# A two-block layer kernel: five changed waits in the first block, three weight low halves by an adding DMA, six selection rounds inside the sparse attention

## What is computed

```python
proj = h @ w_in                                   # h: normed, modulated x, [512, 1024]
ssm_u, ssm_z, q, k, v, attn_z, q_idx, k_idx, w_idx = jnp.split(proj, split_points, axis=-1)
y_ssm = s5_mixer(ssm_u, ...) * jax.nn.silu(ssm_z)     # a state space scan, then a gated linear unit
# dsa_mixer: score = sum over 8 index heads of w_idx * relu(q_idx . k_idx), causal;
#            the 128 best keys of each query; softmax(q . k / 8 + bias) over those keys; times v
y_attn = dsa_mixer(q, k, v, q_idx, k_idx, w_idx, ...) * jax.nn.silu(attn_z)
x = x + gate * (jnp.concatenate([y_ssm, y_attn], -1) @ w_out)
```

## Time and profile before

| | |
|---|---|
| median of 3 runs | 1530.57 us (1530.06 to 1534.65) |
| span of the profiled execution | 1522.9 us |
| TensorE busy | 1484.2 us (97%) |
| VectorE busy | 828.6 us (54%) |
| ScalarE busy | 604.1 us (40%) |
| GpSimd busy | 20.7 us (1%) |
| mean granted TensorE clock | 0.996 of full speed |

### The profile page before, as it was taken

The page is one execution under the profiler, slowest core; times in us unless marked ns, Lnnn a source line. Parts: engine busy times, 40 slices in busy tenths (PEclk is TensorE's granted clock), DMA queues, the critical chain, the costliest instruction groups (busy, mean ns, idle before and its releaser), DMA issues.

```text
span 1522.9 us, 19833 instructions
## 1 busy us (share of the span) xinstructions
PE 1484.2 (97%) x8104; PEld 1203.6 (79%) x8104; DVE 828.6 (54%) x1359; ACT 604.1 (40%) x918; POOL 20.7 (1%) x36
## 2 busy tenths in 40 slices
PE   8999999999999999999999999999999999999997
PEld 6766957668887887888889777888887888888887
DVE  7978987775646663334346343433448544443234
ACT  4355335663336553334336333432334323232220
POOL 0020100000000000000000000000000000000000
PEclk9999999999999999999999999999999999999998
DMA  9531533043221112122222212223331323232221
GB/s 351 174 112 57 115 130 121 28 166 139 99 79 72 56 56 68 71 83 84 100 102 84 84 56 83 83 83 111 138 111 56 111 83 111 83 111 77 104 97 56
DMA packets 24905, 151.69 MB, mean 100 GB/s; under 512 B 3520, under 2 KB 6128, under 8 KB 8800
## 3 DMA queue, kind: packets, MB, share of 16 engines
q1 hardware_dynamic: 22304, 136.71, 24.9%
q0 software_dynamic: 2512, 13.72, 3.3%
HBM read 143.83 MB, written 7.88 MB: 100 GB/s over the span
## 4 chain that ended last, share of the span: by engine, by line
PE 86%; DVE 10%; ACT 2%; issue 1%; DMA 1%; SPq 0%; DVEq 0%; ACTq 0%
PE bank L574 84%; DVE score L2206 1%; DVE small L2205 1%; DMA w_raw<-wstream 1%; PE bank L1021 1%; DVE w_lo L1958 1%; DVE score L2221 1%; DVE tval L1911 1%; PE bank L953 0%; DVE sgb L1918 0%; DVE y_lo L1984 0%; DVE h_lo L1984 0%; DVE tval L2455 0%; ACT w_hi L1288 0%; DVE sgb L2322 0%
## 5 line engine op out<-in xcount | busy, mean ns | idle before, releaser
L574 PE MATMUL bank<-h_hi,w_hi 128*128 128x512 f32 (+1 forms) x1104 | 438.4, 397 | 6.6 <-DVE w_lo L1958 3.1
L574 PE MATMUL bank<-h_hi,w_lo 128*128 128x512 f32 (+1 forms) x1120 | 437.0, 390 | 0.0
L574 PE MATMUL bank<-h_lo,w_hi 128*128 128x512 f32 (+1 forms) x1104 | 430.6, 390 | 0.0
L1958 DVE TENSOR_TENSOR w_lo<-w_raw,w_hi 128x2048 fp32r<-128x2048 f32 (+2 forms) x104 | 234.6, 2256 | 248.9 <-ACT w_hi L1288 247.2
L1288 ACT CAST w_hi<-w_raw 128x2048 fp32r<-128x2048 f32 (+2 forms) x108 | 202.6, 1876 | 139.0 <-PE bank L574 134.8
L574 PEld LDWEIGHTS bank<-h_hi,w_hi 128*128 128x128 f32 (+1 forms) x1104 | 207.1, 188 | 62.3 <-issue 17.9
L574 PEld LDWEIGHTS bank<-h_hi,w_lo 128*128 128x128 f32 (+1 forms) x1120 | 210.3, 188 | 45.3
L574 PEld LDWEIGHTS bank<-h_lo,w_hi 128*128 128x128 f32 (+1 forms) x1104 | 207.3, 188 | 41.6 <-issue 0.2
L574 PE MATMUL bank<-y_hi,w_hi 128*128 128x512 f32 x272 | 108.9, 400 | 1.9 <-DVE y_lo L1984 1.9
L574 PE MATMUL bank<-y_hi,w_lo 128*128 128x512 f32 x272 | 106.1, 390 | 0.0
L574 PE MATMUL bank<-y_lo,w_hi 128*128 128x512 f32 x272 | 105.9, 389 | 0.0
(11 more groups left out here) (401 smaller groups left out, 1821.0 us busy)
## 6 DMA issues: line engine op xcount, KB each, us to landing
w_raw<-wstream SPq DMA_DIRECT2D x119, 1024.0 KB, 4.8
w_raw<-wstream SPq DMA_DIRECT2D x4, 768.0 KB, 4.2
bias_rows<-bias_table POOLq DMA_DIRECT2D x1, 2560.0 KB, 11.2
xr<-xT SPq DMA_DIRECT2D x4, 512.0 KB, 5.2
bias<-bias_rows POOLq DMA_DIRECT2D x1, 2048.0 KB, 12.8
xr<-xT SPq DMA_DIRECT2D x1, 2048.0 KB, 8.4
x_saved<-xr POOLq DMA_DIRECT2D x1, 2048.0 KB, 10.8
xr<-x_saved POOLq DMA_DIRECT2D x1, 2048.0 KB, 8.0
```

Source lines behind the costliest of these rows:

```text
L574: return pe.matmul(out, lhsT, rhs, start=start, stop=stop)
L1958: dve.tensor_tensor(w_low_of(s)[:, 0:kt, :], w_raw[:, i % RAW_SLOTS, 0:kt, :], hi_of(s)[:, 0:kt, :].bitcast(f32), ALU.subtract).then_inc(w ...
```

## The change

1. VectorE: `split_low(2)` stands ahead of `state_inputs`, `split_low(3)` ahead of `input_rows(1)`, `split_low(4)` right behind `chunk_turns`; `output_rows` in two parts around `split_low(5)`.
2. The transposes of `win_re` follow the first tile of `ssm_u`, those of `win_im` stand between the halves of the second, through four banks; ScalarE's copies are moved accordingly.
3. Each quarter of the scan's outputs waits for its own `k_ready` instead of for the fourth.
4. Gate tiles 2, 3 and 4: VectorE's `gate_low` is gone. ScalarE writes the negated high half (as it is rounded on the way out) over the raw half, and GpSimd issues a DMA, two for each tile, that adds the weights from HBM to it. TensorE waits for both DMAs of a tile before it uses it.
5. `silu(az)` becomes x/2 * (1 + tanh(x/2)): ScalarE computes tanh per part (j = 0, 2, 4, 6), VectorE `(tanh + 1) * x` (j = 2, 3, 6, 7), and `attn_gated` multiplies by 0.5 as well; it moves from j = 9 to 10, its low half from 10 to 11.
6. Six of the eleven rounds behind `k_ready` move into the attention, at j = 2, 4, 5, 6, 8 and 9.

```diff
@@ GpSimd, behind the load of the bias
+            for j, n in enumerate(NEGATED):          # NEGATED = (2, 3, 4)
+                i = SPLIT_AT[GATE_TILES[n].s]
+                for part in range(2):
+                    ks = slice(4 * part, 4 * part + 4)
+                    pool.wait_ge(gate_negated, 2 * j + part + 1)
+                    pool.dma_start(w_lo[:, i % RAW_SLOTS, ks, :],
+                                   wstream[i].rearrange("p (t c) -> p t c", c=WC)[:, ks, :],
+                                   accum_op=ALU.add).then_inc(gate_summed[j], 16)
@@ TensorE, gemm_unit, k == 0
+                    if gr in GATE_TILES and GATE_TILES.index(gr) in NEGATED:
+                        pe.wait_ge(gate_summed[NEGATED.index(GATE_TILES.index(gr))], 32)
@@ TensorE, ssm_u
-            for gr in G["ssm_u"]:
-                gemm(gr, "fm", h_hi, h_lo)
-            pe.wait_ge(win_ready, 1)
-            for b in range(8):
-                src = (win_re, win_im)[b // 4]
-                if b >= 2:
-                    pe.wait_ge(wint_act, b - 1)
+            def input_turns(part):
+                if part == 0:
+                    pe.wait_ge(win_ready, 1)
+                src = (win_re, win_im)[part]
+                for b in range(4):
+                    if part:
+                        pe.wait_ge(wint_act, b + 1)
...
+            gemm(G["ssm_u"][0], "fm", h_hi, h_lo)
+            input_turns(0)
+            gemm(G["ssm_u"][1], "fm", h_hi, h_lo, between=lambda: input_turns(1))
@@ TensorE, the scan's outputs
-            pe.wait_ge(k_ready, 4)
...
             for q in range(4):
+                pe.wait_ge(k_ready, q + 1)
@@ TensorE, ahead of out1
+            pe.wait_ge(gate_summed[-1], 32)
@@ ScalarE, ssm_u
             for w, gr in enumerate(G["ssm_u"]):
                 ahead(gr)
+                if w:
+                    input_turned(0)
...
                     elif half == 0:
                         cosine(cos_t[:, :, :]).then_inc(rotation_ready, 1)
+                        input_turned(1)
@@ ScalarE, gate_high
+                act.activation(w_low_of(s)[:, ks, :], w_raw[:, i % RAW_SLOTS, ks, :], ACT.Copy, scale=-1.0)\
+                   .then_inc(gate_negated, 1)
@@ ScalarE, attention
+            def gate_tanh(m):
+                if m >= 2:
+                    act.wait_ge(tanh_used, m - 1)
+                act.activation((root, rstd)[m % 2][:, :], az[:, m, :], ACT.Tanh, scale=0.5).then_inc(tanh_ready, 1)
...
-                if j == 7:
-                    gate_silu(az, range(4))
-                if j == 9:
+                if j == 10:
                     attn_high(0)
                     attn_high(1)
@@ VectorE, the start
+            split_low(2)
             state_inputs()
             input_rows(0)
-            split_low(2)
+            split_low(3)
             input_rows(1)
             dve.nop().then_inc(win_ready, 1)
-            split_low(3)
             chunk_turns()
+            split_low(4)
...
-            output_rows(0, 1)
-            split_low(4)
-            output_rows(1, 3)
+            output_rows(0, 2)
             split_low(5)
-            output_rows(3, 4)
+            output_rows(2, 4)
@@ VectorE, behind k_ready
-            select_keys(11)
+            select_keys(11 - len(SELECTED))          # SELECTED = (2, 4, 5, 6, 8, 9)
@@ VectorE, attention
+            def gate_finished(m):
+                dve.wait_ge(tanh_ready, m + 1)
+                dve.scalar_tensor_tensor(out=az[:, m, :], in0=(root, rstd)[m % 2][:, :], scalar=1.0, in1=az[:, m, :],
+                                         op0=ALU.add, op1=ALU.mult).then_inc(tanh_used, 1)
...
+                if j == 2:
+                    dve.nop().then_inc(w_low, len(NEGATED))
+                if j in SELECTED:
+                    select_keys(1)
+                if j in GATE_FINISHED:               # {2: 0, 3: 1, 6: 2, 7: 3}
+                    gate_finished(GATE_FINISHED[j])
```

More of the change, by code:

```diff
@@ L36 @@
 BIAS_LEN = 640
+NEGATED = (2, 3, 4)
 D_FF = 2816
@@ L309, in hybrid_blocks @@
         ki_copied, ki_doubled, wi_ready, wi_row, wi_psum, mod_row, gate_row = sem("ki_copied"), sem("ki_doubled"), sem("wi_ready"), sem("wi_row"), sem("wi_psum"), sem("mod_row"), sem("gate_row")
-        az_ready = sem("az_ready")
+        az_ready, tanh_ready, tanh_used = sem("az_ready"), sem("tanh_ready"), sem("tanh_used")
         x_act, kr_psum, k_ready, heads_loaded = sem("x_act"), sem("kr_psum"), sem("k_ready"), sem("heads_loaded")
@@ L328, in hybrid_blocks @@
         sc_psum, a_ready, o_psum, o_copied = sem("sc_psum"), sem("a_ready"), sem("o_psum"), sem("o_copied")
-        gate_ready = sem("gate_ready")
+        gate_ready, gate_negated = sem("gate_ready"), sem("gate_negated")
+        gate_summed = [sem(f"gate_summed{j}") for j in range(len(NEGATED))]
         on_ready, dec_loaded = sem("on_ready"), sem("dec_loaded")
@@ L467, in hybrid_blocks @@
         GATE_HIGH = {2: (2, 0), 3: (2, 1), 6: (3, 0), 7: (3, 1), 11: (4, 0), 12: (4, 1)}
-        GATE_LOW = {0: ((1, 0), (1, 1)), 1: ((1, 2), (1, 3)), 4: ((2, 0), (2, 1)), 5: ((2, 2), (2, 3)),
-                    8: ((3, 0), (3, 1)), 9: ((3, 2), (3, 3)), 13: ((4, 0), (4, 1)), 14: ((4, 2), (4, 3))}
+        GATE_LOW = {0: ((1, 0), (1, 1)), 1: ((1, 2), (1, 3))}
+        SELECTED = (2, 4, 5, 6, 8, 9)
         GATE_UNITS = [4] * 8 + [3] * 8
         GATE_DONE = {0: 0, 2: 1, 4: 2, 6: 3, 8: 4, 11: 5, 14: 6, 15: 7}
+        GATE_FINISHED = {2: 0, 3: 1, 6: 2, 7: 3}
         RET_FILL = [(gr, half) for name in ("ret_q", "ret_k", "ret_v") for gr in G[name] for half in range(2)]
@@ L778, in _ @@
             gemm(G["q_idx"][1], "fm", h_hi, h_lo)
-            for gr in G["ssm_u"]:
-                gemm(gr, "fm", h_hi, h_lo)
-            pe.wait_ge(win_ready, 1)
-            for b in range(8):
-                src = (win_re, win_im)[b // 4]
-                if b >= 2:
-                    pe.wait_ge(wint_act, b - 1)
-                for i in range(4):
-                    ins = pe.transpose(bank[5 + b % 2][:, i * P:i * P + P], src[:, 4 * (b % 4) + i, :], ident)
-                ins.then_inc(wint_psum, 1)
+            def input_turns(part):
[5 more added lines that the diff above has]
+                        pe.wait_ge(wint_act, b + 1)
+                    for i in range(4):
+                        ins = pe.transpose(bank[4 + b][:, i * P:i * P + P], src[:, 4 * b + i, :], ident)
+                    ins.then_inc(wint_psum, 1)
+            gemm(G["ssm_u"][0], "fm", h_hi, h_lo)
+            input_turns(0)
+            gemm(G["ssm_u"][1], "fm", h_hi, h_lo, between=lambda: input_turns(1))
             def relevance(i0, i1):
@@ L1405, in _, with input_turned @@
             act.nop().then_inc(copied_act, 1)
+            def input_turned(part):
+                dst = (win_re, win_im)[part]
+                for b in range(4):
+                    act.wait_ge(wint_psum, 4 * part + b + 1)
+                    act.copy(dst[:, 4 * b:4 * b + 4, :],
+                             bank[4 + b][:, :].rearrange("p (i c) -> p i c", c=P)).then_inc(wint_act, 1)
             for w, gr in enumerate(G["ssm_u"]):
                 ahead(gr)
+                if w:
+                    input_turned(0)
                 for half in range(2):
@@ L1614, in _ @@
                     gate_half(GATE_DONE[j])
+                    if GATE_DONE[j] < 4:
+                        gate_tanh(GATE_DONE[j])
                 if j in GATE_HIGH:
                     gate_high(*GATE_HIGH[j])
-                if j == 7:
-                    gate_silu(az, range(4))
-                if j == 9:
+                if j == 10:
                     attn_high(0)
@@ L2347, in attn_gated @@
                 rows = slice(qt * P, qt * P + P)
-                dve.wait_ge(az_ready, 1)
+                dve.wait_ge(tanh_used, 4)
                 a = y_attn(qt)
@@ L2355, in attn_gated @@
                     out = by_tile(bank[PV_BANK][:, :])
-                dve.tensor_tensor(by_tile(new_val(a)), out, az[:, :, rows], ALU.mult).then_inc(act_val, 1)
+                dve.scalar_tensor_tensor(out=by_tile(new_val(a)), in0=out, scalar=0.5, in1=az[:, :, rows],
+                                         op0=ALU.mult, op1=ALU.mult).then_inc(act_val, 1)
                 if qt >= 2:
@@ L2366, in ssm_gated @@
             def ssm_gated(m):
-                dve.wait_ge(az_ready, 2 + m // 3)
+                dve.wait_ge(az_ready, 1 + m // 3)
                 dve.tensor_tensor(new_val(y_ssm(m)), z32[:, m, :], sz[:, m, :], ALU.mult).then_inc(act_val, 1)
@@ L2389, in _ @@
                     gate_low(*part)
-                if j == 9:
+                if j == 2:
[4 more added lines that the diff above has]
+                    gate_finished(GATE_FINISHED[j])
+                if j == 10:
                     attn_gated(0)
                     attn_gated(1)
-                if j == 10:
+                if j == 11:
                     attn_low(0)
```

## The result

The changed kernel takes **1515.7 us** (median of 4 runs, 1515.31 to 1516.44) against 1531.42 us (1530.06 to 1534.65) for the kernel before beside it: ratio 0.9905, 95% interval 0.9886 to 0.9923. On another chip it was 1515.98 against 1529.75, 0.9909 (0.9894 to 0.9924).

What follows compares the result with a forecast made beforehand. TensorE, busy 97% of the span, was taken as the bound, with VectorE's list behind each wait. Gains of 3.95 (start), 3.2 (k_ready) and 2.4 (attention) made 9.55 us: 1530.57 - 9.5 = 1521.0 us, range 1517.5 to 1526.5.

Steps and rivals of the forecast that it cites:

- Start, TensorE's side: Up to relevance: 3.1 us wait for split_low(2) goes, turns take 4.1 to 4.2 us; relevance 5.1 us earlier, at 91.9.
- Start, what is late next: Behind relevance: second relu and VectorE's list come later, new TensorE wait 1.1 to 1.2 us, leaving 3.95 us gained.
- k_ready: Scan's outputs, wait at 204.53 us: no quarter waits, gain 3.2 us; six moved rounds keep that gain.
- Attention: Attention, j = 7 to 11: waits of 2.0 and 0.7 us go, 0.3 lost; net 2.4 us, bounds 0.5 to 3.2.
- Adding DMA: Gate tiles 2 to 4: a part lands in 5 to 6.5 us, within 10.2 us or more of cover, no wait.
- the rivals on it: Adding DMA slower than its cover: by a little (10%), 1524.5 us; by much (6%), 1539 us at a landing of 18.
- the one slower than before: Rival, 6%: adding DMA much slower, TensorE waits at tiles 2, 3 and `out1`; 1539 us at a landing of 18 us.
- tanh: Attention: 0.6 us in each of four iterations, no table load; rival (4%): two 1.28 us loads each, 1524 to 1527 us.
- the last of the sum: Span to time: span 1522.9 becomes 1513.4; the median's 7.7 us above the span carried over, giving 1521.0 us.
- more than the sum: Rival, 8%: the end of the attention and the new wait at 94 us also go; 1518.5 us.
- the wait at 94 us: After four relevances and six matmuls: TensorE's new wait of 1.1 to 1.2 us for the second relu, there at 95.2.
- the tight iterations: Attention, such as j = 2, 6, 9, 11: little or no slack left; lower bound 0.5 us if each loses a few tenths.

Runs made afterwards that it cites:

- the 69: Runs of the kernel before, unchanged, whose span is known; a straight line through them gives 1.03 us for each 0.001 of clock.
- one experiment of three: Constant products in TensorE's waits: four waits of the kernel before, 1527.58 us; changed kernel's k_ready wait put back, 1521.11 and 1521.26; its 1131 to 1136 us, 1514.10.

## Why the prediction was right, and where not

- **Start, TensorE's side.** Relevance was forecast at 91.9 and began at 91.89. That this agrees to 0.01 us is luck, for two errors cancel. The second `q_idx` tile began at 55.45 instead of 55.0, as everything from the first low part on is 0.5 us later than in the profile of before; the turns of `win_re`, forecast at 76.9, came at 77.34 for the same reason. And the turns hold TensorE for 91.89 - 55.45 - 32.7 = 3.7 us instead of 4.1 to 4.2: the forecast took four times the 1.03 us of a group of eight, a duration that overlaps the next work. There is no wait for ScalarE's copies. VectorE's new idle time was put at 1.1 us and is 1.02.
- **Start, what is late next.** The new wait for a relu exists, 0.76 us instead of 1.1 to 1.2. The first score begins at 96.14, forecast 95.7.
- **k_ready.** The outputs were to begin at 204.53 - 3.23 - 3.95 = 197.35 and began at 197.25, by the same two errors: the start brought 4.5 us, not 3.95, and 0.5 was lost ahead of it. No quarter waits, and from 120 to 205 us TensorE is busy 84.06 of 85 us. VectorE's idle time ahead of `y_lo` is 7.24 us, forecast at least 6; the prediction's own numbers, 1.38 + 9.1 - 3.2, give 7.3 and not the "some 8" in its text. Undoing part 6 makes the first `y_lo` 1.7 us late, forecast 1.8.
- **Attention.** Of the waits for line 2383, 0.5 us stay, forecast 0.3. Between 197 and 318 us TensorE gains 9.42 - 7.28 = 2.1 us, forecast 2.4. One small wait was not seen: 0.51 us at 231.19, since ScalarE, earlier now, stands 2.21 us for raw weights ahead of that tile's high half.
- **Adding DMA.** Landing 5.3 to 5.8 us, forecast 5 to 6.5, with no wait; the rivals on it fell, the one slower than before among them. The hold-off by VectorE that the Trainium skill describes ("DMA: Bandwidth & Descriptors", "SWDGE vs HWDGE vs iDMA") is not to be seen in six landings that lie within 0.5 us; whether VectorE worked in that mode beside them, no run here shows.
- **tanh.** ScalarE loads a table at 231.15 and the next at 307.94, with the tanh parts between them, 0.63 us each. The Trainium skill's placing of tanh and exp in one set ("ScalarE: Activation LUTs", "Table sets: the hidden batching unit") agrees with this trace.

```profile
231.15 1.28 ACT L1632 ACT_TABLE_LOAD   x1 [0.17 <-ACT sgb L1561]
307.94 1.28 ACT L1606 ACT_TABLE_LOAD   x1
```

- **The step that failed** is the last of the sum: "the median lies 7.7 us above the span, and I carry that over". The profile of before had one low-clock window and 0.996; the runs of before have 0.992 in the mean, and only one of the 69 is above 0.995. I treated 7.7 us as a constant around the span, when 1.8 are constant and 5.9 depend on the clock. The step also took for granted that an after-profile would be just as quick against its own runs. The changed kernel's profile is ordinary for it: 1515.31 against a median of 1515.7. With 1.8 us the same sum would have given 1513.4 + 1.8 = 1515.2 us. None of the rivals held this step up to question; the one that pointed below the forecast, "more than the sum" at 1518.5 us, named the wait at 94 us, which stayed, and the end of the attention.
- **What the runs put in its place**: 1.8 us between span and time, about 10.6 us of difference at equal clock (9.9 by the marks of the profiles), and about 2.8 us that go with the clock: the changed kernel runs at 0.995 instead of 0.992. The two differences make 13.4 of the 13.8 to 15.7 us measured. That a low stretch costs time is shown (1.6 us between fixed marks); that the removed stops are the reason for the higher clock is argued, and filling the stops bore it out in one experiment of three by times.

**What stays open.** Why one stop is followed by the lower clock in one execution and not in the next; and whether each removed stop has a share of its own in the 2.8 us (with one wait filled there was no low window behind it, but one at 430 us, and no gain). Four profiles of before against two of after are too few to settle these. The Trainium skill, "TensorE: Matmul & The Clock Gate", Part 1, says that what the clock gate watches runs freely and isn't set by the start of a kernel; that would fit the changing places, but no run here shows it.

## What to carry to other kernels

Before a span is turned into a time, compare time and span run by run: what is constant may be carried over, and the rest belongs to the execution that was profiled, to be placed by its mean granted clock among the runs. Compare marks inside a kernel from a common event, not from the start of the span: here that told a true gain of 4.5 us from the 3.95 forecast, where the raw time agreed by luck. In this kernel, in which TensorE is busy 97% of the time, the change gave back more than the waits' length and the clock was higher, though no run shows that the one follows from the other; filling a wait with idle work was no sure substitute. When an edit removes a wait, ask in the same breath what is late next: here that one question (relus, VectorE's slack at `y_lo`, the tight iterations) gave each wait that was forecast to within 0.4 us.

## What the hardware showed that was not expected

- One kernel, unchanged, ran from 1523.2 to 1535.3 us, one core on each of four chips, in step with a mean granted clock of 0.997 to 0.987: about 1 us for each 0.001.
- A stretch at the lower clock between fixed marks cost 1.6 us (55.89 instead of 54.28 us).
- The same 3.2 us stop at 201 us was followed by the lower clock in one profile and not in another; low windows lay at 20, 60, 200, 440, 790 and 1150 us, in changing choice.
- A GpSimd DMA that adds 512 KB from HBM to float32 in place lands in 5.6 us (5.3 to 5.8); the same DMA copying takes 4.0.
